# Twelve of sixteen merge-gate tiles computed as Strassen-Winograd products of half size

## What is computed

```
z = rmsnorm(x) @ w_in[l]          # q, k, v of three branches, branch gates, S5 input u, and g_a, g_s (1024 columns each)
o_a = three-branch attention(q, k, v);   o_b = s5(u)
merged = sigmoid(g_a) * (o_a @ proj_nsa) + sigmoid(g_s) * (o_b @ proj_s5)
x = x + merged @ w_out
x = x + experts(rmsnorm(x))       # 32 experts in 4 groups; one group, two experts a token
```

## Time and profile before

| | |
|---|---|
| median of 3 runs | 1857.74 us (1856.37 to 1858.37) |
| profiled execution | 1859.41 us, its span 1857.7 us |
| granted TensorE clock, mean over the span | 0.971 |
| instructions | 21432 |
| HBM read and written | 489 MB and 30 MB |

### The profile page before, as it was taken

The page is one execution under the profiler, slowest core; times in us unless marked ns, Lnnn a source line. Parts: engine busy times, 40 slices in busy tenths (PEclk is TensorE's granted clock), DMA queues, the critical chain, the costliest instruction groups (busy, mean ns, idle before and its releaser), DMA issues. The chain is left out here.

```text
span 1857.7 us, 21432 instructions
## 1 busy us (share of the span) xinstructions
PE 1691.3 (91%) x7466; PEld 820.3 (44%) x7466; DVE 552.8 (30%) x1678; ACT 392.0 (21%) x967; POOL 81.6 (4%) x157
## 2 busy tenths in 40 slices
PE   8999999999998778788999999999999987787878
PEld 6664554455443333233477645544544433333333
DVE  4872345335000000000378713553340000000003
ACT  3322454011111111111132234540111111110111
POOL 1000000000010000000000000000001100000100
PEclk9999999999999989998999999999999999998999
DMA  5641100463999999999938211004659999999998
GB/s 168 151 139 46 46 23 23 181 249 135 398 428 427 427 425 427 427 427 428 389 103 222 68 46 46 23 23 181 249 201 411 428 427 426 426 427 428 426 427 336
DMA packets 121904, 496.40 MB, mean 267 GB/s; under 512 B 42036, under 2 KB 78900, under 8 KB 94160
## 3 DMA queue, kind: packets, MB, share of 16 engines
q1 hardware_dynamic: 109584, 472.75, 64.1%
q0 software_dynamic: 8928, 16.52, 2.4%
q10 hardware_dynamic: 3296, 5.84, 0.8%
HBM read 489.25 MB, written 30.47 MB: 280 GB/s over the span
## 5 line engine op out<-in xcount | busy, mean ns | idle before, releaser
L1104 PE MATMUL bank<-arena 128*64 128x512 f32 x2176 | 695.0, 622 | 89.2 <-DMA arena<-in_expert_up 33.6
L1104 PEld LDWEIGHTS bank<-arena 128*64 128x64 f32 x2176 | 230.4, 143 | 354.4 <-issue 354.2
L2033 DVE SCALAR_TENSOR_TENSOR arena<-bank,halves,arena 128x512 f32<-128x512 f32 x32 | 24.0, 751 | 813.9 <-PE bank L1104 813.9
L779 PE MATMUL bank<-hT,arena 128*128 128x512 f32 x512 | 258.8, 609 | 2.6 <-ACT arena L1343 2.5
L1104 PE MATMUL bank<-h,arena 128*64 128x512 f32 x320 | 140.3, 614 | 25.4 <-DMA arena<-in_expert_gate 9.2
L1104 PE MATMUL bank<-spare_slot,arena 128*64 128x512 f32 x320 | 136.3, 624 | 28.8 <-ACT arena L1492 10.6
L1104 PE MATMUL bank<-hT,arena 128*64 128x512 f32 x256 | 123.6, 640 | 0.0
L756 PE MATMUL bank<-arena,hT 128*128 128x256 f32 (+1 forms) x512 | 119.3, 390 | 3.5 <-DMA arena<-in_w_in 2.8
L997 PE MATMUL bank<-arena,hT 128*128 128x512 f32 x256 | 115.0, 597 | 0.0
L779 PEld LDWEIGHTS bank<-hT,arena 128*128 128x128 f32 x512 | 84.3, 192 | 56.0 <-issue 50.6
L756 PEld LDWEIGHTS bank<-arena,hT 128*128 128x128 f32 x512 | 96.8, 192 | 19.8 <-issue 3.0
(11 more groups left out here) (366 smaller groups left out, 1638.5 us busy)
## 6 DMA issues: line engine op xcount, KB each, us to landing
arena<-in_expert_up SPq DMA_DIRECT2D x48, 2048.0 KB, 41.1
arena<-in_expert_gate SPq DMA_DIRECT2D x44, 2048.0 KB, 35.1
arena<-in_expert_down SPq DMA_DIRECT2D x44, 2048.0 KB, 41.5
arena<-in_w_in SPq DMA_DIRECT2D x26, 1024.0 KB, 7.6
spare_slot<-in_expert_gate SPq DMA_DIRECT2D x8, 2048.0 KB, 29.8
h<-in_expert_gate SPq DMA_DIRECT2D x8, 2048.0 KB, 31.6
hT<-in_expert_up SPq DMA_DIRECT2D x8, 2048.0 KB
spare_slot<-in_expert_down SPq DMA_DIRECT2D x8, 2048.0 KB, 37.6
```

Source lines behind the costliest of these rows:

```text
L779: r = pe.matmul(bank[:, FB, :], lhs, rhs, start=(k == 0), stop=last)
L1104: r = pe.matmul(dst[CAP * e:CAP * e + CAP, :], moving[:, k, CAP * e:CAP * e + CAP], w, start=(k == 0), stop=(k == n - 1))
L2033: STT(hid, bank[:, 3, :], slot_root, hid, ALU.mult, ALU.mult).then_inc(act_ready, 1)
```

## The change

Gate tiles are taken in pairs. The first two pairs (`PLAIN` = 2) stay as they are. In the other six (`FAST`), the 1024x256 weights are cut into 2x2 blocks of 512x128 and the tokens into 2x2 blocks of 512x256, and the pair is computed from seven products in Winograd's form instead of eight block products. A product is four matmul calls of 128x256. So:

- TensorE: 28 calls of 256 columns for a pair instead of 16 of 512. Two products share the bank, one in each half; a group of two is eight calls. `fill(cost)` counts a 256-column call as 1 and a 512-column one as 2. In the S5 outputs a `fill(2)` stands behind the first part of each step only; `FILL_AT` is written anew.
- VectorE: four differences of token blocks (`token_sums`, 128x1024 each) between `chunk_scan` and `sums_qk(NT)`, one of them in place in `hT`, which waits for the plain tiles; and seven sums of 128x256 for each pair (`half_sums`), in `add_fills` at the end of a unit.
- GpSimd: four sums of weight blocks for each pair (`weight_sum`, 128x512 each).
- ScalarE: a copy of each group of two products from the bank to `fast_p` (two buffers), which waits until the sums of the group before are done; Tanh of each finished pair in place in `gates` three half-units later (`tanh_fast`). The table switch between the first two fill copies goes.
- The ring: fast chunks use slots 0 and 2, their weight sums the slots 1 and 3. A fast chunk is loaded once the pair two before it is done. The last half of `proj_nsa` waits for the last pair.
- The merge no longer waits for the last fill copy on TensorE; VectorE waits for `gate_ready` at every second tile. SP's first expert load, which overwrites `fast_p`, waits for all half sums.

```diff
+PLAIN = 2
+FAST = 8 - PLAIN
+C_FAST = 5 + PLAIN
+RING_AT = [0, 1, 2] + [3, 3] + [3, 2] + [0, 2] * (FAST // 2) + [1, 0, 2]
...
-FILL = [("gate", i) for i in GATES[:12]] + [("z", m) for m in range(4)] + [("gate", i) for i in GATES[12:]]
+ORDER = (1, 6, 2, 7, 4, 5, 3)
+PRODUCTS = [(j, n) for j in range(FAST) for n in ORDER]
+FILL = [("gate", i) for i in GATES[:2 * PLAIN]] + [("fast", g) for g in range(14)]
+for m in range(4):
+    FILL += [("z", m), ("fast", 14 + m)]
+FILL += [("fast", g) for g in range(18, len(PRODUCTS) // 2)]
...
-FILL_AT = [4, 3, 3, 3, 3, 3,
-           3, 3, 3, 3, 3, 1,
-           1, 1, 1, 2, 2, 1,
-           2, 2, 1, 3, 3, 3]
+FILL_LAST = 2
+FILL_AT = [8] + [6] * 11 + [2, 6] * 4 + [2, 2, 6, 2]
...
+        FACTORS = {1: ("a11", "b11"), 6: ("s2", "t2"), 2: ("a12", "b21"), 7: ("s3", "t3"), 5: ("s1", "t1"),
+                   4: ("a22", "t4"), 3: ("s4", "b22")}
...
+                    out_, x1, x2, op = {1: ("s1", "a21", "a22", ALU.add), 2: ("s2", "s1", "a11", ALU.subtract),
+                                        3: ("s3", "a11", "a21", ALU.subtract), 4: ("s4", "a12", "s2", ALU.subtract)}[n]
+                    pool.tensor_tensor(out=w[out_], in0=w[x1], in1=w[x2], op=op).then_inc(w_sums, 1)
...
                 sp.wait_ge(sT_ready, 2)
+                sp.wait_ge(half_sum, len(HALF_SUMS))
...
+                dst, w, h = bank[:, FB, HALVES[half]], fast_weights(j)[a][:, k, :], fast_tokens()[b][:, k]
+                if n == 4:
+                    dst = dst.rearrange("p (b d) -> p b d", b=2)
+                return pe.matmul(dst, w, h, start=(half == 0 and k == 0), stop=(half == 1 and k == KD // 2 - 1))
...
-                            if part < 2 or i % 2 == 0:
-                                fill(1)
+                            if part == 0:
+                                fill(2)
...
-                fill(FLEN[0] * len(FILL))
-                pe.wait_ge(fill_evac, len(FILL))
+                fill(2 * KD * len(FILL))
...
+                if kind == "fast":
+                    if m >= 2:
+                        act.wait_ge(half_sum, sums_through(m - 1))
+                    r = act.activation(fast_p[m % 2], bank[:, FB, :], ACT.Copy)
...
+                    if n == 6:
+                        r = TT(first[:, LATE], product(j, 1), p, ALU.add)
+                    elif n == 2:
+                        r = TT(first[:, EARLY], product(j, 1), p, ALU.add)
+                    elif n == 7:
+                        r = TT(second[:, LATE], first[:, LATE], p, ALU.add)
+                    elif n == 4:
+                        r = TT(second[:, EARLY], second[:, LATE], p, ALU.add)
+                    elif n == 5:
+                        TT(first[:, LATE], first[:, LATE], p, ALU.add).then_inc(half_sum, 1)
+                        r = TT(second[:, LATE], second[:, LATE], p, ALU.add)
+                    else:
+                        r = TT(first[:, LATE], first[:, LATE], p, ALU.add)
...
                 chunk_scan()
+                token_sums(1, 2)
+                token_sums(4, 3)
                 sums_qk(NT)
```

More of the change, by code:

```diff
@@ L109, in fill_steps @@
 def fill_steps():
-    at = list(itertools.accumulate(x for n in FILL_AT for x in (n, 1)))
-    ends = [sum(FLEN[:i + 1]) - FILL_AHEAD for i in range(len(FILL))]
+    at = list(itertools.accumulate(x for n in FILL_AT for x in (n, FILL_LAST)))
+    ends = [e - FILL_AHEAD for e in itertools.accumulate(fill_cost(g) for g in FILL)]
     return [next((n for n, d in enumerate(at) if d >= e), len(at)) for e in ends]
@@ L117, with product_at, fast_done, tanh_at @@
 GATE_S5_AT = FILL_STEP[FIDX[("z", 3)]] // 2 + 1
+HALF_SUMS = [(j, n, k) for j, n in PRODUCTS for k in range({1: 0, 5: 2}.get(n, 1))]
+SUM_AT = {x: i + 1 for i, x in enumerate(HALF_SUMS)}
 def fills_ending(step):
     return [i for i in range(FILLED, len(FILL)) if FILL_STEP[i] == step]
+def product_at(j, n):
+    return PRODUCTS.index((j, n))
+def fast_done(j):
+    return FIDX[("fast", product_at(j, 3) // 2)] + 1
+def tanh_at(step):
+    return [j for j in range(FAST) if FILL_STEP[fast_done(j) - 1] + 3 == step]
+def sums_through(g):
+    return max(i for x, i in SUM_AT.items() if x[:2] in PRODUCTS[2 * g:2 * g + 2])
 def key_tiles(unit):
@@ L218, in trunk @@
         ring = [view(8 * i, KD * CW) for i in range(NRING)]
+        fast_w = [view(16 * i, KD, CW) for i in range(2)]
+        fast_s = [[view(16 * i + 8 + 2 * k, KD // 2, P) for k in range(3)] for i in range(2)]
         gates = view(32, 16, S)
@@ L492, in lay, with ring_count @@
             return ap[bass.ds(l, 1), :, :, :].rearrange("o g m n -> (o g) m n")
+        def ring_count(c):
+            return sum(16 * HEADS if CHUNKS[i][0] == "proj_nsa" else 16 for i in range(c + 1) if RING_AT[i] == RING_AT[c])
         block = ctx.enter_context(nc.Block())
@@ L761, in _, with fast_product, fill @@
             filled = [0, 0]
-            def fill(n):
-                for left in range(n, 0, -1):
+            def fast_product(j, n, k):
+                if n == 1 and k == 0:
+                    chunk(C_FAST + j)
+                elif n == 6 and k == 0:
+                    pe.wait_ge(h_sums, 2)
+                    pe.wait_ge(w_sums, 4 * j + 2)
+                elif n == 7 and k == 0:
+                    pe.wait_ge(h_sums, 4)
+                    pe.wait_ge(w_sums, 4 * j + 3)
+                elif n == 3 and k == 0:
+                    pe.wait_ge(w_sums, 4 * j + 4)
+                a, b = FACTORS[n]
+                half = product_at(j, n) % 2
+                dst, w, h = bank[:, FB, HALVES[half]], fast_weights(j)[a][:, k, :], fast_tokens()[b][:, k]
+                if n == 4:
+                    dst = dst.rearrange("p (b d) -> p b d", b=2)
+                return pe.matmul(dst, w, h, start=(half == 0 and k == 0), stop=(half == 1 and k == KD // 2 - 1))
+            def fill(cost):
+                while cost > 0 and filled[0] < len(FILL):
                     i, k = filled
-                    if i == len(FILL):
-                        return
                     kind, m = FILL[i]
@@ L782, in fill @@
                     filled[:] = [i + 1, 0] if last else [i, k + 1]
-                return 0
+                    cost -= each
             def group(g, tap=None):
@@ L1348, in evac_fill, with tanh_fast, evac_fills @@
                 r.then_inc(fill_evac, 1)
+            def tanh_fast(j):
+                act.wait_ge(half_sum, SUM_AT[j, 3, 0])
+                for k in range(2):
+                    g = gates[:, fast_gates(j) + k, :]
+                    act.activation(g, g, ACT.Tanh, scale=0.5).then_inc(gate_ready, 1)
+            def evac_fills(step):
+                for i in fills_ending(step):
+                    evac_fill(i)
+                for j in tanh_at(step):
+                    tanh_fast(j)
             def table_of(function, n):
@@ L1473, in _ @@
                         evac_heads(n)
-                for i in fills_ending(2 * len(UNITS)):
-                    evac_fill(i)
+                for step in range(2 * len(UNITS), 2 * len(UNITS) + 4):
+                    evac_fills(step)
                 enter(act, exp_clear, l)
@@ new lines, in half_sums @@
+                def half_sums(j, n):
+                    m = fast_gates(j)
+                    first, second = gates[:, m, :], gates[:, m + 1, :]
+                    i = product_at(j, n)
+                    p = product(j, n)
+                    dve.wait_ge(fill_evac, FIDX[("fast", i // 2)] + 1)
+                    if n in (7, 3):
+                        dve.wait_ge(half_sum, SUM_AT[j, {7: 6, 3: 5}[n], 0])
+                    elif n in (4, 5):
+                        dve.wait_ge(half_sum, SUM_AT[j, 7, 0])
+                    if n == 6:
[9 more added lines that the diff above has]
+                        r = TT(second[:, LATE], second[:, LATE], p, ALU.add)
+                    else:
+                        r = TT(first[:, LATE], first[:, LATE], p, ALU.add)
+                    r.then_inc(half_sum, 1)
@@ L1821, in _ @@
                 do(TS(gsig, gsig, 1.0, 0.5, ALU.add, ALU.mult))
+                for g in range(2):
+                    group_sums(g)
                 def gate_s5():
```

114 lines of the change are left out of this document (87 added, 27 removed).

## The result

The changed kernel takes **1835.61 us**, the median of four runs (1832.27 to 1837.06), against 1857.05 for the kernel before (four runs, 1855.56 to 1858.37). The ratio is 0.9877, with a 95% interval of 0.9864 to 0.9889. It is 21.4 us faster. 29.2 were forecast, so nearly 8 are missing. The profiled execution took 1836.43 us, its span is 1834.7.

The account below looks back on a forecast made before the run. TensorE bounds the stages ahead of the experts, weight traffic the experts. A layer saves 15.4 + 0.7 - 0.1 - 0.3 - 0.5 - 0.6 = 14.6, two 29.2: forecast 1828.5 us, own range 1824 to 1834, 8 in 10 1824 to 1840.

Parts of the forecast that it names:

- rival 1: Attention units: they lose their cover and half of the added VectorE and ScalarE work shows, 7 to 10 us a layer; chance 0.12.
- Rival 2: Scan: GpSimd's sums hold the shared port against VectorE, 7.0 us a layer at 2.3 a sum, 2.6 at 1.2; chance 0.06.
- Rival 3: Ahead of the compressed keys: VectorE's token differences delay them, 2.7 us a layer, 1834 us; chance 0.05.
- the stated signs of being wrong: TensorE standing for VectorE's differences or compressed keys, scan rows beyond 1.23 us, or a bank-copy wait at each group.
- S5 stretch, 15.4 saved a layer: S5 outputs: 20 fills become 8 and two bank waits go, so the stretch takes 15.4 us instead of 30.8.
- The step that failed: GpSimd's weight sums, 1.2 us each: ready before they are wanted, hidden at both ends, no cost of their own.
- Units: Attention units: under 0.3 us for halved calls, net 0.5 for late turns, 0.6 held back for GpSimd's sums meeting VectorE, a layer.
- The merge: Start of the merge: the 0.7 us wait for the last copy is dropped; later transfers of weights cost nothing.
- rival 4: Single fill bank: TensorE stands at each group's end; gain gone at 0.70 us an end, 1870 us at 1.0; chance 0.04.
- rival 5: Halved matmul rows pay for their weight loads, 0.043 us on each of 336 rows, so no change; chance 0.03.

Follow-up runs that it names:

- the first experiment: Changed kernel, with GpSimd waiting until VectorE has finished the compressed keys before the second fast pair's weight sums: 1827.39 us, ratio 0.9832 against the kernel before.
- the zeros: Changed kernel with each GpSimd weight sum replaced by a memset of zeros in the same place, output not the reference's: 1827.41 us, one run.
- the copies: Changed kernel with GpSimd's four sums of the second fast pair replaced by copies of one operand: 1829.64 us, one run.
- the quarters: Changed kernel with GpSimd's four sums of the second fast pair cut into 16 instructions of 128x128: 1827.64 us, ratio 0.9841 against the kernel before.
- TensorE kept busy: Changed kernel with three useless matmul calls into an unused bank ahead of the turn of the compressed keys: 1835.06 us, ratio 0.987 against the kernel before.
- the two units mended: Changed kernel with GpSimd's second sums behind the keys, plus VectorE's sums of units 19 and 22 and `gate_s5` behind the next `weigh`: 1824.7 us, ratio 0.9823.

## Why the prediction was right or wrong

The sign and the main mechanism were right; the size was off by 7 us. The forecast's own range, 1824 to 1834, did not hold the time. The wide one, to 1840, did, and it had been stretched for rivals 1 to 3: one of them came about. One of the stated signs of being wrong came true as well: TensorE stood for the compressed keys.

- **S5 stretch, 15.4 saved a layer.** Steps and price of a matmul were right: without the wait the stretch takes 15.86 us, forecast 15.4. In the changed kernel it took 20.16, so 10.7 were saved.
- **The step that failed** is that of GpSimd's sums: "At both ends they are hidden and cost nothing of their own", with 0.6 a layer held back for a meeting "in a unit without cover". I asked when the sums are wanted and when they can be done, not what VectorE does in between. Their price was nearly right (1.2 forecast, 1.29 measured), and so was the slack of the keys' chain (1.4 us behind its start; in the first experiment 1060.11 + 1.33 = 1061.44 against `tkc` at 1062.90, so 1.5). The sums stretched the chain from 1.33 to 5.34 us: 4.0 less the 1.4 to spare is the wait, nearly (2.6 against 2.7).
- **Rival 2 came true at another place.** I had put the held port over the scan, with the first pair's sums. Those met VectorE too, but cost it 0.8 us in one row, since the others beside them read PSUM (L1920 to L1923 above), and the scan still ended 2.2 us ahead of the stretch. The second pair's landed on eight short rows that TensorE waits for, and four of these were held for one sum each: a short row pays as much as a long one. The rival's own arithmetic, four sums less 2.2, gives 3.0 at 1.29 a sum, near the 2.7. The Trainium skill's "SBUF — State Buffer", Who interferes with whom, says that GpSimd and VectorE lock each other out of the port that they share; the zeros (nothing held), the copies and the quarters (held to each instruction's end) agree with that. What I gave 0.06 should have had about a third, as I judge it now: a stated lock, two engines newly at work together, and a chain with 1.4 us of slack.
- **No rival had the clock.** A wait of 2.7 us cost another 1.7 through the lower clock behind it. Both together are 4.4 of the 4.8 us that are missing in the stretch.
- **Units.** Forecast 0.3 for halved calls, 0.5 for stalls and 0.6 held back, 1.4 together; measured 155.80 against 154.84 (155.53 less the wait of 0.69 ahead of the merge), 0.96 more. That the sums are near is partly luck, for the parts don't all agree. Unit 23's late turns were right (0.7, forecast 0.65). In unit 20 `gate_s5`, 1.29 us, stood between the copies and `weigh`, which I had missed: 1.3 us. Unit 14 was to lose 0.4 and lost nothing (1.22 before, 1.23 after), and unit 16 lost 0.5 that nobody forecast (0.61, then 1.11). Against it the turn of unit 17 was short again, as forecast (1.22, then 0.61), and so were those of units 11, 13 and 19 (1.02, 1.11 and 0.79 before). GpSimd's sums lie over the units too, at four places. They held rows there (L2041 at 1115.72, 1.19 us instead of 0.17), and no wait of TensorE came of it.
- **The merge.** Its wait is gone, 0.7, and nothing of the later transfers shows: right.
- **Rivals 1, 3, 4, 5.** The units kept their cover (0.96 instead of 7 to 10). Rival 3 fell by experiment. No wait for the fill bank is left from the S5 stretch to the merge, where rival 4 needed 0.70 at each group. The halved fills of the S5 stretch take 1.06 us to the next part's start (1070.41 to 1071.47 with TensorE kept busy); less 0.19 for the switch, that is 0.217 for each of four rows, and a weight load is not to be seen in it.

The ledger of the second layer, row to row: before 318.55, after 308.11, with the sums behind the keys 303.80, with the two units mended 301.78. The second step is 4.3 us a layer and brings the gain to 14.75; 14.6 was forecast. That these two agree so well is partly luck: the stretch without the wait took 0.4 us more than forecast, and the units 0.4 less.

## What to carry to other kernels

When work is given to GpSimd, ask which VectorE instructions run during it, not only whether it is done in time: one that reads SBUF may be held to the end of the GpSimd instruction, however short it is itself. Here rows with one operand in PSUM were not held. So keep GpSimd away from chains of short rows that another engine waits for, by a wait on the chain's end, or cut its instructions small (quarters of a sum gave the same time as moving them, 1827.6 and 1827.4 us). And count a wait of TensorE of 2 to 3 us with what comes behind it.

## What the hardware showed that I had not expected

- A VectorE row of 16 columns, 0.16 us alone, took 1.14 to 1.24 beside sums of 1.29, and 0.47 to 0.57 beside copies of 0.65. Setting zeros (0.54 each) held nothing. A TENSOR_SCALAR of 96 columns, with one operand in SBUF, was held as well (1.33 instead of 0.21).
- Some rows between slip through at full speed (L1821 at 1069.80 and 1069.88, 0.16 and 0.15): two short ones pass, then the next is held, and the same two passed beside copies and beside quarters. Why those and not the others, no run here shows.
- A sum of 128x512 takes 1.29 us on GpSimd, of 128x128 0.45 to 0.47: a quarter of the size costs over a third of the time.
- After 2.7 us without a matmul the granted clock was 0.66 and 0.70 in the next two windows, 5.3 us together; with matmuls in that place it did not fall.
